# A two-layer transformer on one core: layer 1's output gate moved into the second weights, the last norm done tile by tile, attention's transposes moved behind the scores

## The reference, cut to what matters

```python
x = _layer_norm(DEEPNORM_ALPHA * x + g_a * y, ln1_g[l], ln1_b[l])
x = _layer_norm(DEEPNORM_ALPHA * x + g_m * _squared_relu_mlp(x * (1 + sc_m) + sh_m, mlp_w1[l], mlp_w2[l]),
                ln2_g[l], ln2_b[l])

def _squared_relu_mlp(h, w1, w2):
    return jnp.square(jax.nn.relu(h @ w1)) @ w2
```

## Time and profile before

| | |
|---|---|
| median of 3 runs | 3066.44 us (3064.03 to 3069.26) |
| the profiled execution, its own time | 3066.85 us |
| its span, first to last instruction | 3065.1 us |
| PE busy | 2793.9 us, 91% of the span |
| DVE busy | 1376.0 us, 45% |
| ACT busy | 878.4 us, 29% |
| POOL busy | 512.2 us, 17% |
| mean granted TensorE clock | 0.956 of 2.4 GHz |

### The profile page before, as it was taken

One profiled execution on the slowest core, in us unless ns is written; L12 is line 12 of the kernel. 1 busy time (PEld: TensorE's weight loads), 2 busy tenths in 40 slices (PEclk: granted clock), 3 DMA queues, 4 the chain that ended last, 5 costly groups with the idle time before them and its releaser, 6 DMA issues. The chain is left out here.

```text
span 3065.1 us, 40504 instructions
## 1 busy us (share of the span) xinstructions
PE 2793.9 (91%) x15572; PEld 2287.0 (75%) x15572; DVE 1376.0 (45%) x2159; ACT 878.4 (29%) x1669; POOL 512.2 (17%) x355
## 2 busy tenths in 40 slices
PE   5999993999999999999948999999698999999993
PEld 2666773778888888888836888888587888888882
DVE  3575536573333333333482555555555333333336
ACT  4233323342121121211143433443442122112211
POOL 0000002332121121121230000000042222122214
PEclk6999996999999999999968999999899999999996
DMA  6574215441011010110132111100452111111113
GB/s 219 193 302 161 73 51 182 140 130 55 27 41 41 27 55 27 41 41 27 42 130 81 40 44 36 42 29 8 131 131 83 41 55 49 47 41 55 52 44 110
DMA packets 193648, 239.42 MB, mean 78 GB/s; under 512 B 15977, under 2 KB 154817, under 8 KB 187393
## 3 DMA queue, kind: packets, MB, share of 16 engines
q1 hardware_dynamic: 193248, 237.81, 24.3%
q10 hardware_dynamic: 288, 0.10, 0.0%
HBM read 204.22 MB, written 37.88 MB: 79 GB/s over the span
## 5 line engine op out<-in xcount | busy, mean ns | idle before, releaser
L2005 DVE TENSOR_TENSOR y<-y,pair 128x1024 f32<-128x1024 f32 x288 | 351.2, 1220 | 338.2 <-PE pair L2083 338.2
L2081 PE MATMUL pair<-m_wbh,m_ath 128*128 128x512 f32 x1152 | 449.8, 390 | 4.6 <-DVE y L2005 4.5
L2083 PE MATMUL pair<-m_wbh,m_atl 128*128 128x512 f32 x1152 | 450.3, 391 | 0.0
L2082 PE MATMUL pair<-m_wbl,m_ath 128*128 128x512 f32 x1152 | 449.4, 390 | 0.0
L2033 DVE TENSOR_TENSOR m_atl<-m_sq,m_ath 128x512 fp32r<-128x512 f32 x160 | 102.9, 644 | 672.7 <-POOL m_sq L1929 671.8
L1903 ACT ACTIVATE m_rel<-pair 128x512 f32<-128x512 f32 x160 | 88.9, 556 | 996.8 <-PE pair L2105 989.9
L1929 POOL TENSOR_TENSOR m_sq<-m_rel 128x512 f32<-128x512 f32 x160 | 155.6, 973 | 1206.3 <-ACT m_rel L1903 1206.1
L2103 PE MATMUL pair<-hth,m0n_wah 128*128 128x512 f32 (+1 forms) x768 | 272.4, 355 | 2.8 <-ACT m_rel L1903 2.7
L2105 PE MATMUL pair<-hth,m0n_wal 128*128 128x512 f32 (+1 forms) x768 | 272.7, 355 | 0.0
L2104 PE MATMUL pair<-htl,m0n_wah 128*128 128x512 f32 (+1 forms) x768 | 272.6, 355 | 0.0
L2081 PEld LDWEIGHTS pair<-m_wbh,m_ath 128*128 128x128 f32 x1152 | 216.3, 188 | 52.8 <-DVE y L2005 7.5
(11 more groups left out here) (250 smaller groups left out, 5101.3 us busy)
## 6 DMA issues: line engine op xcount, KB each, us to landing
a_ring<-in_w_mod SPq DMA_DIRECT2D x40, 1024.0 KB, 9.0
m_rawb<-in_mlp_w SPq DMA_DIRECT2D x64, 512.0 KB, 4.2
m_rawa<-in_mlp_w SPq DMA_DIRECT2D x60, 512.0 KB, 4.2
x_rows<-r_res SPq DMA_DIRECT2D x28, 512.0 KB, 3.1
r_raw<-cat_cols SPq DMA_DIRECT2D x18, 512.0 KB, 4.9
m_rawa<-x_rows SPq DMA_DIRECT2D x18, 512.0 KB, 3.8
mod_w<-in_w_mod SPq DMA_DIRECT2D x8, 1024.0 KB, 12.2
r_xin<-in_x SPq DMA_DIRECT2D x16, 512.0 KB, 3.6
```

Of the source, the lines that this page charges most:

```text
L2005: dve.tensor_tensor(k.y[:, t, :], k.y[:, t, :], k.pair[t % 2][:, :], ALU.add).then_inc(s_y, 1)
L2081: pe.matmul(o, ath[:, m, ts], wbh[:, m, cols], start=m == 0, stop=False)
L2082: pe.matmul(o, ath[:, m, ts], wbl[:, m, cols], start=False, stop=False)
L2083: i = pe.matmul(o, atl[:, m, ts], wbh[:, m, cols], start=False, stop=m == M - 1)
```

## The change

Four things are done.

- In layer 1 the gate row is multiplied into the second weights: POOL multiplies each `rawb` half by `growt` (the row, spread over the partitions) in place in every step, in group 1 before that group's squares, and ACT's split waits for POOL (`s_bg`) where it waited for the DMA.
- `y` begins as 1.41 times the residual: SP loads `x_dram`'s rows into `y` when the first part of the block is through (6 tiles, then the last 2 behind the last store), and DVE scales them in place of the memsets (`begin_y`).
- `stage_rows(1, 2)` is gone. In `stage_block(1)` DVE's last addition of a tile also gives its sum (L2005 becomes a reduce), a small operation makes the negative mean, ACT sums the squares of the centred tile and takes the root, DVE applies both rows and SP stores the tile at once. The loop has DVE's sum of tile t ahead of the finish of tile t-1.
- In attention PE's `turn(n-1)` stands directly behind `scores(n)`, the job is cut in two halves of four k-tiles with `turn_values` between them, DVE's `values_in` comes behind `normalise`, and ACT's `evacuate(n-1)` always comes ahead of `exps(n)`.

```diff
 # attention, PE
                     scores(n)
+                if n:
+                    if n - 1 in turn_step:
+                        pe.wait_ge(s_v, values_before[turn_step[n - 1]] + 1)
+                    turn(n - 1)
+                if n in at_step:
+                    job(at_step[n], 0, KT // 2)
                 if n in turn_step:
-                    if n >= 2:
-                        pe.wait_ge(s_pb, n - 1)
+                    pe.wait_ge(s_pb, n)
                     turn_values(turn_step[n], TB)
                 if n in at_step:
-                    job(at_step[n], 0, KT - 2)
-                if n:
-                    if n in turn_step:
-                        pe.wait_ge(s_v, values_before[turn_step[n]] + 1)
-                    turn(n - 1)
-                if n in at_step:
-                    job(at_step[n], KT - 2, KT)
+                    job(at_step[n], KT // 2, KT)
...
 # block, SP
+                if final and t == tiles - 1:
+                    sp.wait_ge(s_yps, tiles)
+                    sp.wait_ge(s_dve, C * t + 1)
+                    sp.dma_start(growt.rearrange("p (j q) -> p j q", q=P),
...
+                    for u in range(tiles - 2):
+                        sp.dma_start(k.y[:, u, :], rows(k.x_dram, u, True)).then_inc(s_yx[u], 16)
...
+            if final:
+                for i in range(2):
+                    sp.wait_ge(s_store[i], 16 * len(range(i, tiles, 2)))
+                for u in range(tiles - 2, tiles):
+                    sp.dma_start(k.y[:, u, :], rows(k.x_dram, u, True)).then_inc(s_yx[u], 16)
...
 # block, POOL, in a step
                 for g, (a, n) in enumerate(groups):
+                    if final and g == NG - 1:
+                        for m in range(M):
+                            if starts(c):
+                                pool.wait_ge(s_grow, 16)
+                            wait(pool, s_rawb[m], 16 * (c + 1))
+                            pool.tensor_tensor(rawb[:, m, :], rawb[:, m, :], growt, ALU.mult).then_inc(s_bg, 1)
...
 # block, DVE: before the steps, and the end
+                    if final:
+                        dve.wait_ge(s_yx[t], 16)
+                        dve.tensor_scalar(k.y[:, t, :], k.y[:, t, :], ALPHA, None, ALU.mult).then_inc(s_y, 1)
...
-            clear_y(0, 2)
+            begin_y(0, 0 if final else 2)
             split_ht(tiles - 2)
-            clear_y(2, XT)
+            begin_y(0 if final else 2, XT - 2 if final else XT)
             split_ht(tiles - 1)
-            clear_y(XT, tiles)
+            begin_y(XT - 2 if final else XT, tiles)
...
+            def moments_sum(t):
...
+                dve.tensor_tensor_reduce(k.y[:, t, :], k.y[:, t, :], k.pair[t % 2][:, :], 1.0, 0.0,
+                                         ALU.add, ALU.add, stats[:, t % 2, 0, 0:1]).then_inc(s_y, 1)
+                dve.wait_ge(s_y, tiles + n + 1)
+                dve.tensor_scalar(fmv[:, t % 2, 0:1], stats[:, t % 2, 0, 0:1], -1.0 / D, None, ALU.mult).then_inc(s_mom, 1)
+            def finish(t):
...
+                dve.wait_ge(s_centre, t + 1)
+                dve.scalar_tensor_tensor(out=y, in0=y, scalar=fmv[:, t % 2, 0:1], in1=lng2, op0=ALU.add, op1=ALU.mult).then_inc(s_res, 1)
+                dve.wait_ge(s_fstd, t + 1)
+                dve.reciprocal(fstd[:, t % 2, 1:2], fstd[:, t % 2, 0:1]).then_inc(s_frec, 1)
...
+                dve.scalar_tensor_tensor(out=y, in0=y, scalar=fstd[:, t % 2, 1:2], in1=lnb2[:, :], op0=ALU.mult, op1=ALU.add).then_inc(s_fin, 1)
...
 # block, ACT, the end
+                    act.activation(rel[:, :, :].rearrange("p a b -> p (a b)"), k.y[:, t, :], ACT.Square, bias=fmv[:, t % 2, 0:1],
+                                   accum_out=fmv[:, t % 2, 1:2]).then_inc(s_centre, 1)
+                    act.wait_ge(s_centre, t + 1)
+                    act.activation(fstd[:, t % 2, 0:1], fmv[:, t % 2, 1:2], ACT.Sqrt, bias=k.eps[:, 0:1], scale=1.0 / D).then_inc(s_fstd, 1)
...
 # build
-              (stage_rows, (0, 2)), (stage_attention, ()), (stage_block, (1,)), (stage_rows, (1, 2))]
+              (stage_rows, (0, 2)), (stage_attention, ()), (stage_block, (1,))]
```

More of the change, by code:

```diff
@@ L1496, in _ @@
             for n in range(N + 1):
-                late = n in at_step or n in turn_step
-                if n and not late:
+                if n:
                     evacuate(n - 1)
@@ L1501, in _ @@
                     exps(n)
-                if n and late:
-                    evacuate(n - 1)
                 if n in at_step:
@@ L1582, in _ @@
                     maxima(n)
-                if n in turn_step:
-                    values_in(turn_step[n], TB)
                 if n:
@@ L1588, in _ @@
                     normalise(n)
+                if n in turn_step:
+                    values_in(turn_step[n], TB)
                 if n in at_step:
@@ L1748, in stage_block @@
     stats = sb("stats", [P, 2, 2, 6])
+    final = layer == DEPTH - 1
+    if final:
+        growt, lng2, lnb2 = k.y[:, XT, :], k.y[:, XT + 1, :], sb("lnb2", [P, D])
+        fmv, fstd = sb("fmv", [P, 2, 2]), sb("fstd", [P, 2, 2])
     xin = [rawa[:, i, :, :].rearrange("p j q -> p (j q)") for i in range(2)]
@@ L1758, in stage_block @@
     s_gate, s_x, s_gated, s_res, s_mom = sem("gate"), [sem("x0"), sem("x1")], sem("gated"), sem("res"), sem("mom")
+    s_grow, s_lnrow, s_bg, s_fstd, s_fin = sem("grow"), sem("lnrow"), sem("bg"), sem("fstd"), sem("fin")
+    s_yx, s_out, s_centre, s_frec = [sem(f"yx{t}") for t in range(XT)], [sem("out0"), sem("out1")], sem("centre"), sem("frec")
     w1 = io["mlp_w1"][layer].rearrange("(k p) f -> p k f", p=P)
@@ L1825, in _ @@
             over_steps(sp, step)
+            if final:
+                for t in range(tiles):
+                    sp.wait_ge(s_fin, t + 1)
+                    sp.dma_start(rows(k.out[0], t, True), k.y[:, t, :]).then_inc(s_out[t % 2], 16)
+                for i in range(2):
+                    sp.wait_ge(s_out[i], 16 * (tiles // 2))
+                return
             sp.wait_ge(s_alow, M * NCH)
@@ L1893, in step @@
                         for m in range(M):
-                            wait(act, s_rawb[m], 16 * (c + 1))
+                            if final:
+                                wait(act, s_bg, M * c + m + 1)
+                            else:
+                                wait(act, s_rawb[m], 16 * (c + 1))
                             wait(act, s_w2, tiles * c)
@@ L1906, in _ @@
             over_steps(act, step)
+            if final:
+                act.wait_ge(s_sq, J * NCH)
+                for t in range(tiles):
+                    act.wait_ge(s_mom, t + 1)
+                    act.activation(rel[:, :, :].rearrange("p a b -> p (a b)"), k.y[:, t, :], ACT.Square, bias=fmv[:, t % 2, 0:1],
+                                   accum_out=fmv[:, t % 2, 1:2]).then_inc(s_centre, 1)
+                    act.wait_ge(s_centre, t + 1)
+                    act.activation(fstd[:, t % 2, 0:1], fmv[:, t % 2, 1:2], ACT.Sqrt, bias=k.eps[:, 0:1], scale=1.0 / D).then_inc(s_fstd, 1)
         @block.gpsimd
@@ L1954, in first_low, with begin_y @@
                     dve.tensor_tensor(wal[:, m, :, :], raw_first[tiles % 2 ^ m], f32(wah[:, m, :, :]), ALU.subtract).then_inc(s_alow, 1)
-            def clear_y(first, end):
+            def begin_y(first, end):
                 for t in range(first, end):
-                    dve.memset(k.y[:, t, :], 0.0).then_inc(s_y, 1)
+                    if final:
+                        dve.wait_ge(s_yx[t], 16)
+                        dve.tensor_scalar(k.y[:, t, :], k.y[:, t, :], ALPHA, None, ALU.mult).then_inc(s_y, 1)
+                    else:
+                        dve.memset(k.y[:, t, :], 0.0).then_inc(s_y, 1)
             low(0)
@@ L2034, in _ @@
             over_steps(dve, step)
+            if final:
+                dve.wait_ge(s_lnrow, 32)
+                for t in range(tiles + 1):
+                    if t < tiles:
+                        moments_sum(t)
+                    if t:
+                        finish(t - 1)
+                return
             for t in range(tiles + 2):
```

15 lines of the change are left out of this document (14 added, 1 removed).

## The result

The changed kernel takes **3046.15 us** (median of 4 runs, 3042.24 to 3047.7), the kernel before beside it 3067.85 (4 runs, 3064.03 to 3070.76). The ratio is 0.9928, 95% interval [0.9913, 0.9943]: 21.7 us faster, where 27 were forecast (3066.44 less 3039.4). The time lies inside the range of the forecast itself, 3031 to 3047, and 0.15 us above the top of the second range, 3023 to 3046. The profiled execution took 3046.93, its span is 3045.1, 20.0 less than before.

The account below looks back on a forecast made before the run. PE was taken to bound attention and the MLP's steps, DVE alone the last stretch before PE's idle 38.4 us. Terms -34.7 + 12 - 1 - 3.3 = -27; 3066.85 - 27.0 - 0.4 = 3039.4 us, own range 3031 to 3047.

Parts of the forecast that it names:

- the second range: Whole kernel: 3023 to 3046 us, said to hold most of the forecast's case and of DVE coming first at the port.
- the start of the MLP: Between attention and the first second-layer matmuls: scalings replace memsets but wait for loads; -1 us, ends -2 and +5.
- The end: Last norm: DVE period 3.95 us per tile, ACT hidden, POOL's multiplications and bunched stores gone; -34.7 us, ends 32.7 and 36.
- some 33 us before the old end: Sign for the end: DVE's last operation would come this much earlier than the old end.
- The gate at the port: MLP steps: POOL's gate locks the shared port, DVE's low half waits, 0.8 us late in 15 steps; +12 us.
- DVE first: Rival, MLP steps: DVE gets the port first or the low half isn't held; the 12 us go, 3027; chance 0.17.
- POOL twice: Rival, MLP steps: POOL keeps the port for both gates, PE 3.1 us late per step; +47, 3074; chance 0.05.
- Attention: Attention's steps: the products' waits for evacuate, 2.1 + 1.2, go; -3.3 us, ends -6 and +4.
- PE's work is the same: Attention: PE's work was taken as unchanged, with only the turn moving ahead of the job.
- 3.8 to land: Start of the MLP: time for the last store, issued at 2312.9, to land before the last two residual loads.
- both of its signs: Start of the MLP: PE's 7.5 us wait ahead shorter or equal, and no wait for `wbl` before the first `second`.
- The clock rival: Rival, attention: scores and turn together drop the granted clock from 2.4 to 1.2 GHz; 3066 or more; chance 0.02.

Follow-up runs that it names:

- second weights first: The changed kernel with SP issuing step 0's two second-weight loads ahead of the gate's row and the residual tiles: 3042.69 us, ratio 0.9908.

## Why the prediction was right, and where not

The port's mechanism was right; the start of the MLP was wrong. That the sum came near is in part luck: the start's +7.1 lies outside the ends given for it (-2 and +5) and attention's -6.6 outside its own (-6 and +4), with opposite signs.

- **The end** (-34.7; -35.7): right. Period 3.91 for 3.95, ACT hidden, as its doubled square shows. The sign "some 33 us before the old end" is a slip: by the prediction's own sum DVE is done 39.9 us before it, and 33 behind the end's start.
- **The gate at the port** (+12; +11.8): right in mechanism, and in size in part by luck. POOL came first, by 0.08 us, and DVE got the port behind one gate. That cost 0.67 us per step where 0.8 was forecast, 10.0 in 15 steps; the other 1.7 us belong to the start, through the clock behind its wait. Of the 0.67 only 0.36 stands in the wait; the remainder is in PE's busy time, whose first matmul after the wait takes 0.50 instead of 0.39 and goes on less densely. Both rivals on this are out: DVE first by the 2.87, POOL twice by the low half's end, 2987.23, 2.3 us ahead of the second gate's. The gate of double width shows what POOL twice would have cost: PE's waits are 2.55 per step, near the 3.1 of that rival, but its steps take 64.0 us more than before's instead of 47, as PE's busy time grows too; the whole is 3103, where the rival said 3074. "SBUF — State Buffer" of the Trainium skill, under "Who interferes with whom", has an exclusive lock for the whole instruction; the low half that ended 0.55 us behind a 4.59 us gate agrees.
- **Attention** (-3.3; -6.6): the waits as forecast, 3.5, and none for `a_ptt` before step 56. Mis-sized was "PE's work is the same": its busy time fell by 3.1. The lower end, -6, named that saving ("transitions saved by the undivided job") but left it out of the sum. Whether it comes from the undivided job stays open.
- **The start of the MLP** (-1; +7.1): the step that failed. It said "3.8 to land" for the last store, the price of one transfer alone, and let it be issued at 2312.9. It was issued at 2309.59 and landed in 12.0, because six residual tiles and two rows of the norm, 512 KB each, had been issued ahead of it on SP: 4.7 MB, the store included, from 2300.3 to 2321.6. With the loads behind it the store landed in 3.7. The step priced SP's issue order and each load for itself, but not what the loads do to the store and to each other: the six landed 6.7 to 13.9 us behind their issue, and the split behind their scalings came late. And it did not see that ACT's first relu waits for all stores (`act.wait_ge(s_store[i], ...)`, L1909). So both of its signs failed: PE's 7.5 us ahead of the MLP became 9.25, and there was a wait for `wbl`, 3.92. "DMA: Bandwidth & Descriptors" of the Trainium skill, on queues, rings and completion order, says that SP's transfers share one queue whose work each DMA engine takes in order; 12.0, 16.1 and 3.7 agree with that.
- **The first scores** (0; +3.5): scatter of a part that the change does not touch.

The forecast was 5.3 us too fast in the difference: start +8.1, first scores +3.5, attention -3.3 and end -1 make +7 in the profiled pair (20.0 for 27), and the medians lie 1.7 further apart than the spans. The clock rival did not come in attention: 1.00 there, with the transposes now directly behind the scores. Its price was a slip: the 27 us of the forecast are gone at 6% of 474 us on the lower level, not at 8%. The lower level came elsewhere, behind PE's wait for the second weights (1.7 us) and in the kernel with the gate of double width (19.3 us).

## What to carry to other kernels

When a load moves to an earlier place on a queue, price the store that now stands behind it, with all bytes ahead of it, and list who waits for that store. An engine's extra work costs nothing only where it doesn't share the port with work that is due: the same 30 multiplications cost 10.0 us in one place and nothing in the other. When a stretch comes out as forecast, look at where in it the time stands: 1.7 us of the MLP's steps belonged to a wait ahead of them. And before a wait is moved or dropped, look which iteration issues it: in a loop by register the code for "the first step" may never run.

## What the runs showed of the hardware that was not expected

- PE's waits of 0.36 us in 15 steps left the granted clock at 1.00; 12 of 15 waits of 2.6 us were followed by 0.50 for about 3.5 us, which goes with 19.3 us more of busy time beside 32.9 more of waiting. Behind the one wait of 3.92 us (after) the first half step took 12.65, behind one of 1.2 (second weights first) 11.04, and without a wait (before) 10.94.
- A low half released by POOL's own square starts 0.08 us behind POOL's next instruction and loses the port to it (2984.28 and 2984.36; 2416.45 and 2416.53).
- DVE's scaling with a constant, 0.68 us, took 2.83 beside POOL's operations on 128x1024, though it reads only one tensor: three times one scaling came behind one whole operation of POOL. The prediction had reckoned with that for operations of two tensors alone.
